# Second-layer chunk attention: its sixteen heads placed among the q, k, v and output products

## The chip, the cores and the metric

One core of one Trainium2 chip. The metric is device time in microseconds (us) of the whole kernel, median of the runs; lower is better.

## The reference, cut to what matters

Three layers run one after the other on 256 tokens of width 1024: two layers of a first block, then one layer of a second block on 272 tokens. Each has a mixer and a feed-forward network. The change is in the mixer of the second layer, which is chunk attention with 16 heads of 64:

```python
def chunk_band_mixer(u, w_qkv, rel_bias, w_out):
    qkv = (u @ w_qkv).reshape(bsz, n_chunks, CHUNK, 3, C_HEADS, C_DIM)
    q, k, v = qkv[:, :, :, 0], qkv[:, :, :, 1], qkv[:, :, :, 2]
...
    scores = scores + bias.astype(jnp.float32)[None, None]
    p = jax.nn.softmax(jnp.where(valid[None, :, None, None, :], scores, -jnp.inf), axis=-1).astype(v.dtype)
...
    return o.reshape(bsz, seq, MIX_ODD) @ w_out
h = h + chunk_band_mixer(u, od_w_qkv[i], od_rel_bias[i], od_w_out[i])
u = rms_norm(h, g_ffn[layer])
h = h + swiglu(u, w_gate[layer], w_up[layer], w_down[layer])
```

With 256 tokens all earlier chunks lie within reach, so a query sees every key of its own chunk of 64 and of those before. The bias depends on head and distance.

## The kernel before, in words

**Products.** Every weight matrix is cut into units of 1024 x 256. SP loads a unit into one of four `raw` slots; ScalarE (ACT) rounds it to `w_hi` (`split_hi`, L344) and VectorE (DVE) takes the rest as `w_lo` (`split_lo`, L353), each two units ahead of TensorE (PE). `product` (L492 to L494) does three fp32r matmuls for one k-tile: high by high, high by low, low by high. A unit is 2 output halves x 8 k-tiles x 3 = 48 matmuls of 256 columns. I call the three matmuls of one k-tile and half a group; a unit has 16.

**Order.** Each engine runs its own list in the order in which it is written, and semaphores tie the lists. A wait holds back all that stands behind it on its engine. `Phase` numbers the units and says which pair of PSUM banks each writes. `pair_read` counts its evictions, `unit_done` the units, `xl_done` the finished low parts of the moving operand.

**Second mixer.** `ph_qk` (8 units) makes q and k feature-major, evicted by DVE through `scaled` (L938). `ph_v` (4 units) makes v token-major, evicted by ACT (L1329). Then `chk`, an `Attention` object, does the 16 heads alone. Per head: GpSimd (POOL) copies 64 rows of q into the zeroed `q_pad_c` (L793); PE does two fp32 score matmuls and adds the chunk mask to each by a small bf16 matmul (L804, L807); DVE adds the bias (L1797, L1799), takes maxima (L727) and negates (L731); ACT does two exponentials with row sums (L681); DVE takes reciprocals (L740); PE transposes three blocks (L639); ACT copies them (L690); PE multiplies by v (three blocks of 64 columns, L648); ACT writes the scaled output (L699). When all heads are done PE turns the output feature-major with 16 transposes (`turn_pe`, L878), ACT and DVE split it (`o_hi`, `o_lo`), and `ph_out1`, 4 units, multiplies by the output weights.

**Output products.** `residual_dve` and `residual_act` go with `ph_out0` (first layer) and `ph_out1`. After unit k DVE adds it to `h` (L915), ACT makes the high part of the next input (`late_hi`, L925), DVE the low part (`late_lo`, L933), ACT squares (L966), and only then ACT and DVE split the next weights. The feed-forward's first unit needs the bank pair of unit 3. `fold_squares` (POOL, L418) adds up the squares and `late_sums` (PE, L435) sums them over features between the feed-forward's first and second unit.

## Time and profile before

| | us |
|---|---|
| median of 3 runs | 1218.66 (1216.96 to 1220.9) |
| profiled execution, its own time | 1217.98 |
| its span | 1216.2 |
| PE busy in it | 1152.9 |
| DVE, ACT, POOL busy | 784.1, 578.2, 55.5 |
| mean granted TensorE clock | 0.973 |

Busy times are sums over the span. Since PE is busy nearly throughout, the length of a stage is read from the chain that ended last, and a change has to be followed to what PE waits for. Times below are from the span's start.

### The profile page before, as it was taken

Reading aid. Unit: us, or ns where it says so; the run is one execution under the profiler, and the core shown is the slowest. Engines: PE = TensorE matmul, PEld = TensorE weight load, DVE = VectorE, ACT = ScalarE, POOL = GpSimd, SP = SyncE. Lnnn points to the kernel's source line nnn. Section 1 sums busy time; section 2 is a strip of 40 time slices with the busy share of each in tenths; the row PEclk is TensorE's granted clock in tenths of the full one; section 3 lists DMA queues with packets and bytes.
Section 4 is the critical chain, followed back from the end, with each engine's and each line's share of the span. In section 5 each row is a group of like instructions: output and inputs, shape, how many; then the busy total and the mean of one; then the engine's idle time right before and its main releaser. Section 6 shows DMA issues by size and latency. Waiting matters only on the chain.

```text
span 1216.2 us, 22867 instructions
## 1 busy us (share of the span) xinstructions
PE 1152.9 (95%) x9061; PEld 1110.9 (91%) x9061; DVE 784.1 (64%) x1224; ACT 578.2 (48%) x838; POOL 55.5 (5%) x82
## 2 busy tenths in 40 slices
PE   5998899999999999999999899999899998999998
PEld 4997899999999979999999799888687998999997
DVE  4546655655655475555555587989887666778743
ACT  4546654444444376444444443332355636565531
POOL 0003010000010020000000000100200000000000
PEclk9999799999999999999999998989898999999999
DMA  7662055654578512565546464333320544555360
GB/s 226 204 187 70 12 162 186 195 165 141 181 257 260 174 35 88 164 200 174 162 157 202 135 178 153 112 119 96 121 74 32 166 151 138 177 168 185 124 211 36
DMA packets 190773, 181.74 MB, mean 149 GB/s; under 512 B 20911, under 2 KB 189116, under 8 KB 190699
## 3 DMA queue, kind: packets, MB, share of 16 engines
q1 hardware_dynamic: 190171, 178.61, 46.4%
q0 software_dynamic: 528, 2.10, 0.6%
q8 instruction: 52, 0.85, 0.3%
q14 instruction: 22, 0.18, 0.0%
HBM read 179.64 MB, written 1.05 MB: 149 GB/s over the span
## 4 chain that ended last, share of the span: by engine, by line
PE 83%; DVE 9%; ACT 5%; issue 1%; DMA 1%; SPq 1%; POOL 0%; DVEq 0%; ACTq 0%; POOLq 0%
PE ps L492 24%; PE ps L493 24%; PE ps L494 24%; PE ps L648 3%; DVE w_lo L353 3%; DVE work L1830 2%; PE ps L804 2%; ACT w_hi L344 2%; PE ps L639 1%; PE ps L878 1%; DMA conv_rows<-in_conv_dw_w 1%; PE ps L1636 1%; PE ps L401 1%; ACT u_hi L925 0%; DVE rope L851 0%
## 5 line engine op out<-in xcount | busy, mean ns | idle before, releaser
L492 PE MATMUL ps<-u_hi,w_hi 128*128 128x256 f32 (+2 forms) x1864 | 534.4, 287 | 18.4 <-DVE u_lo L461 8.7
L493 PE MATMUL ps<-u_lo,w_hi 128*128 128x256 f32 (+2 forms) x1864 | 531.2, 285 | 0.0
L494 PE MATMUL ps<-u_hi,w_lo 128*128 128x256 f32 (+2 forms) x1864 | 530.2, 284 | 0.0
L353 DVE TENSOR_TENSOR w_lo<-raw,w_hi 128x2048 fp32r<-128x2048 f32 (+5 forms) x184 | 385.1, 2101 | 205.2 <-ACT w_hi L344 204.9
L492 PEld LDWEIGHTS ps<-u_hi,w_hi 128*128 128x128 f32 x1864 | 356.6, 191 | 21.5 <-issue 14.8
L494 PEld LDWEIGHTS ps<-u_hi,w_lo 128*128 128x128 f32 x1864 | 356.7, 191 | 0.0
L493 PEld LDWEIGHTS ps<-u_lo,w_hi 128*128 128x128 f32 x1864 | 356.1, 191 | 0.5
L344 ACT ACTIVATE w_hi<-raw 128x2048 fp32r<-128x2048 f32 (+5 forms) x184 | 319.7, 1754 | 48.1 <-PE ps L494 48.1
L493 PE MATMUL ps<-a_lo,w_hi 128*128 128x256 f32 x528 | 148.3, 281 | 0.0
L494 PE MATMUL ps<-a_hi,w_lo 128*128 128x256 f32 x528 | 147.9, 280 | 0.0
L492 PE MATMUL ps<-a_hi,w_hi 128*128 128x256 f32 x528 | 147.3, 279 | 0.1
L492 PEld LDWEIGHTS ps<-a_hi,w_hi 128*128 128x128 f32 x528 | 99.5, 188 | 0.3 <-DVE w_lo L353 0.3
L1830 DVE SCALAR_TENSOR_TENSOR work<-cin,conv_w,work 128x258 f32<-128x258 f32 x240 | 99.6, 487 | 0.0
L494 PEld LDWEIGHTS ps<-a_hi,w_lo 128*128 128x128 f32 x528 | 99.5, 188 | 0.0
L493 PEld LDWEIGHTS ps<-a_lo,w_hi 128*128 128x128 f32 x528 | 99.2, 188 | 0.0
L418 POOL TENSOR_TENSOR work<-work 128x512 f32<-128x512 f32 (+1 forms) x15 | 19.6, 1307 | 733.3 <-ACT work L961 462.4
L991 ACT ACTIVATE a_hi<-act_a 128x512 f32 (+1 forms) x22 | 13.9, 632 | 74.2 <-DVE act_a L1011 74.2
L988 ACT ACTIVATE act_g<-act_g 128x512 f32<-128x512 f32 x22 | 13.9, 632 | 60.1 <-DVE act_g L938 60.1
L961 ACT ACTIVATE work<-h (+2 forms) x24 | 9.0, 417 | 70.3 <-DVE h L915 70.3
L494 PE MATMUL ps<-w_hi,u_lo 128*128 128x256 f32 (+1 forms) x136 | 38.7, 285 | 0.0
L493 PE MATMUL ps<-w_lo,u_hi 128*128 128x256 f32 (+1 forms) x136 | 38.7, 285 | 0.0
L995 DVE TENSOR_TENSOR a_lo<-act_a,a_hi 128x512 f32 (+1 forms) x33 | 22.8, 691 | 24.4 <-ACT a_hi L991 19.0
(266 smaller groups left out, 1305.0 us busy)
## 6 DMA issues: line engine op xcount, KB each, us to landing
raw<-in_w_in SPq DMA_DIRECT2D x24, 1024.0 KB, 5.4
raw<-in_w_gate SPq DMA_DIRECT2D x22, 1024.0 KB, 5.3
raw<-in_w_up SPq DMA_DIRECT2D x22, 1024.0 KB, 5.3
raw<-in_ffn_up SPq DMA_DIRECT2D x22, 1024.0 KB, 5.0
raw<-in_w_down SPq DMA_DIRECT2D x16, 768.0 KB, 4.7
raw<-in_od_w_qkv SPq DMA_DIRECT2D x12, 1024.0 KB, 7.5
raw<-in_w_down SPq DMA_DIRECT2D x16, 640.0 KB, 4.6
raw<-in_ev_w_in SPq DMA_DIRECT2D x8, 1024.0 KB, 8.1
```

Of the source, the lines that this page charges most:

```text
L344: nc.scalar.activation(w_hi[t % RING][:, 0:n], raw[t % RAW][:, 0:n], ACT.Copy).then_inc(hi_done, 1)
L353: nc.vector.tensor_tensor(w_lo[t % RING][:, 0:n], raw[t % RAW][:, 0:n], w_hi[t % RING][:, 0:n].bitcast(F32), ALU.subtract).then_inc(lo_don ...
L418: nc.gpsimd.tensor_tensor(first, first, paired(work)[:, j, :, 0:n], ALU.add).then_inc(sem("sq_folded"), 1)
L492: nc.tensor.matmul(out_ap, a_h, b_h, start=start and n == 0, stop=False)
L493: nc.tensor.matmul(out_ap, a_h, b_l, start=False, stop=False)
L494: mm = nc.tensor.matmul(out_ap, a_l, b_h, start=False, stop=stop and n == len(pairs) - 1)
L648: mm = nc.tensor.matmul(self.O(e, b), self.PT(e, b, key), v(n, e, b, key), start=key == 0, stop=key == len(keys) - 1)
L804: nc.tensor.matmul(out_ap, lhs, rhs, start=t == 0, stop=False)
L988: nc.scalar.activation(act_g[:, s], act_g[:, s], ACT.Silu).then_inc(sem("silu_done"), 1)
L991: nc.scalar.activation(paired(a_hi)[:, j], act_a[:, s], ACT.Copy).then_inc(sem("ffn_hi"), 1)
L995: nc.vector.tensor_tensor(paired(a_lo)[:, j], act_a[:, s], paired(a_hi)[:, j].bitcast(F32), ALU.subtract)\
L1830: nc.vector.scalar_tensor_tensor(out=work[:, tile, 0:NF], in0=src, scalar=tap, in1=work[:, tile, 0:NF], op0=ALU.mult, op1=ALU.add).then_in ...
```

## The change

The twelve units of q, k and v become one phase `ph_qkv` in the order q, k, v for each group of four heads, and the heads are written into the lists at positions counted in groups of three matmuls: position 16k is where unit k begins, 192 is the first output unit. `CK_HEADS` gives a head's scores (40, 52, 64, 76, 88, ... 172, then 184, 192, 200, 208), `CK_TURNS` its transposes (18 positions later, 15 for the last four), `CK_VALUES` its values (4 more). Each other engine has the same loop over positions x with its own share. Units 1 to 11 use one PSUM bank each. The chunk mask is added to the bias table once by POOL, and the mask matmuls go. POOL also normalises the probabilities (two `tensor_scalar` a head). Values are multiplied with v as the stationary operand, padded with zeros to 128 columns (`v_even`, `v_odd`), so that the output comes feature-major and the 16 transposes go. The first three output units run their k-tiles 0 to 5 first, with heads between, and their tiles 6 and 7 together at the end; unit 3 follows. Additions, splits and squares there have an order of their own. `residual_act` in the first layer's `ph_out0` splits the next weights before the late part, and does the late part one unit behind.

```diff
-    ph_qk = Phase(plan, 8, 4, first=1)
-    ph_v = Phase(plan, 4, 4)
+    ph_qkv = Phase(plan, 12, 12, pairs=3)
...
+    GROUPS = 2 * KT
+    EARLY = 2 * (KT - 2)
+    def ck_start(k):
+        return GROUPS * k if k < 12 else GROUPS * 12 + EARLY * (k - 12)
+    CK_HEADS = [GROUPS * (3 * (n // 4) + 2) + 8 + (12 if n < 12 else 8) * (n % 4) for n in range(C_H)]
+    CK_TURNS = [at + (18 if n < 12 else 15) for n, at in enumerate(CK_HEADS)]
+    CK_VALUES = [at + 4 for at in CK_TURNS]
+    CK_END = CK_VALUES[-1] + 4
+    CK_STARTS = {ck_start(k): k for k in range(15)}
+    def due(table, x, late=0):
+        return [n for n, at in enumerate(table) if at + late == x]
...
+        def late_part(i, k, j):
+            for t in range(2):
+                added(i, k, j, t)
+                late_hi(late, j, t)
+            for t in range(2):
+                squares(j, t)
+        one_behind = late is not None and group == 1
         for i, k in ph.steps(nc.scalar):
             split_hi(ph, i, k)
-            if k % group == group - 1:
+            if one_behind:
+                if k:
+                    late_part(i, k - 1, k - 1)
...
-        pairs_read(pool, ph_v)
-        pad_heads(chk, q_c, q_pad_c)
+        nc.gpsimd.memset(v_odd[:], 0.0).then_inc(sem("v_zeroed"), 1)
+        pool.wait_ge(sem("v_zeroed"), 1)
+        pool.wait_ge(sem("ss_done"), norm_at["mix1"][0] + 1)
+        nc.gpsimd.memset(v_even, 0.0).then_inc(sem("v_zeroed"), 1)
+        pool.wait_ge(sem("v_zeroed"), 2)
+        pool.wait_ge(sem("bias_landed"), 16)
+        own = bias_h[:, :, 0:P]
+        nc.gpsimd.tensor_tensor(own, own, c("chunk_mask")[:, ::-1].unsqueeze(1).to_broadcast([P, C_H, P]), ALU.add)\
+            .then_inc(sem("bias_masked"), 1)
+        pool.wait_ge(sem("bias_masked"), 1)
+        def ck_pad(n):
+            k = 3 * (n // 4)
+            pool.wait_ge(pair_read[ph_qkv.pair(k)], ph_qkv.used_before(0, k) + 1)
+            wait(pool, sem("ck_scores"), n - 3)
+            rows = slice(64 * (n % 2), 64 * (n % 2) + 64)
+            nc.gpsimd.tensor_copy(q_pad_c[rows, n % 4, :], q_c[rows, n // 2, :]).then_inc(sem("ck_pad"), 1)
+            pool.wait_ge(sem("ck_pad"), n + 1)
+        ck_pad(0)
+        for n in range(C_H):
+            if n + 1 < C_H:
+                ck_pad(n + 1)
+            pool.wait_ge(sem("ck_rsum"), n + 1)
+            for b, (lo, hi) in enumerate(CK_SPANS):
+                nc.gpsimd.tensor_scalar(p3[:, n % 2, lo:hi], p3[:, n % 2, lo:hi], stat3[:, n % 4, 3, b:b + 1], None, ALU.mult)\
+                    .then_inc(sem("ck_norm"), 1)
+                pool.wait_ge(sem("ck_norm"), 2 * n + b + 1)
...
+        def ck_v(k):
+            g, p = k // 3, ph_qkv.pair(k)
+            act.wait_ge(unit_done, ph_qkv.unit(0, k) + 1)
+            act.wait_ge(sem("v_zeroed"), 2)
+            act.wait_ge(sem("tok_copied"), 1)
             for b in range(2):
-                a = nc.scalar.activation(v_c[:, b, k * UC:(k + 1) * UC], ps[:, 2 * p + b, 0:UC], ACT.Copy, scale=rstd_tok[:, b:b + 1])
+                src = qkv_banks(k)[:, b, :].rearrange("p (j e d) -> p j e d", j=2, e=2)
+                for e, v in enumerate((v_even, v_odd)):
+                    a = nc.scalar.activation(v[:, b, 2 * g:2 * g + 2, HD * e:HD * e + HD], src[:, :, e, :], ACT.Copy,
+                                             scale=rstd_tok[:, b:b + 1])
...
+        for x in range(CK_END):
+            if (k := CK_STARTS.get(x)) is not None and k < 14:
+                if k and k % 3 == 0:
+                    ck_v(k - 1)
+                split_hi(ph_qkv if k < 12 else ph_out1, 0, k if k < 12 else k - 12)
+                if k == 0:
+                    late_roots("mix1")
+            for n in due(CK_HEADS, x, 5):
+                ck_exps(n)
+            for n in due(CK_TURNS, x, 1):
+                ck_copies(n)
+            for n in due(CK_VALUES, x, 1):
+                if n % 2:
+                    ck_out_hi(n // 2)
...
+        split_hi(ph_out1, 0, 2)
+        for j in range(3):
+            out1_hi(j)
+        split_hi(ph_out1, 0, 3)
+        out1_squares(0)
+        out1_hi(3)
+        for j in range(1, 4):
+            out1_squares(j)
...
+        def ck_scores(n):
+            k = 3 * (n // 4) + 1
+            pe.wait_ge(pair_read[ph_qkv.pair(k)], ph_qkv.used_before(0, k) + 1)
+            pe.wait_ge(sem("ck_pad"), n + 1)
+            wait(pe, sem("ck_biased"), n - 1)
+            nc.tensor.matmul(ck_bank(n)[:, 0:P], q_pad_c[:, n % 4, 0:P], k_c[:, n // 2, 0:P], start=True, stop=True)
+            nc.tensor.matmul(ck_bank(n)[:, P:CK_W], q_pad_c[:, n % 4, P:T1], k_c[:, n // 2, :], start=True, stop=True)\
+                .then_inc(sem("ck_scores"), 1)
+        def ck_turns(n):
+            pe.wait_ge(sem("ck_norm"), 2 * n + 2)
+            wait(pe, sem("ck_ptc"), n)
+            for at in range(0, CK_W, P):
+                mm = nc.tensor.transpose(ps[:, 5, at:at + P], p3[:, n % 2, at:at + P], ident)
+            mm.then_inc(sem("ck_pt"), 1)
+        def ck_values(n):
+            j, k, v = n // 2, 3 * (n // 4) + 2, v_odd if n % 2 else v_even
+            pe.wait_ge(pair_read[ph_qkv.pair(k)], ph_qkv.used_before(0, k) + 1)
+            pe.wait_ge(sem("tok_copied"), 1)
+            pe.wait_ge(sem("ck_ptc"), n + 1)
+            if j >= 2:
+                pe.wait_ge(sem("xl_done"), split_at["o1"] + j - 1)
+            out_ap = ps[:, 6 + j % 2, 0:T1]
+            every, later = (out_ap, v[:, 0, j, :], pt3[:, n % 2, 0:T1]), (out_ap[:, P:T1], v[:, 1, j, :], pt3[:, n % 2, T1:CK_W])
+            nc.tensor.matmul(*(later if n % 2 else every), start=n % 2 == 0, stop=False)
+            nc.tensor.matmul(*(every if n % 2 else later), start=False, stop=n % 2 == 1).then_inc(sem("ck_o"), 1)
+        def ck_steps(x):
+            for n in due(CK_TURNS, x):
+                ck_turns(n)
+            for n in due(CK_VALUES, x):
+                ck_values(n)
+            for n in due(CK_HEADS, x):
+                ck_scores(n)
...
+        pairs_read_after = [ph_qkv.used_after[n] for n in range(3)]
+        for k in range(3):
+            begin_unit(ph_out1, 0, k)
+            for t in range(2):
+                if k == 0:
+                    pe.wait_ge(pair_read[t], pairs_read_after[t])
+                elif k == 1 and t == 0:
+                    pe.wait_ge(pair_read[2], pairs_read_after[2])
+                elif k == 1:
+                    pe.wait_ge(sem("ck_biased"), C_H - 1)
+                elif t == 0:
+                    pe.wait_ge(sem("ck_biased"), C_H)
+                else:
+                    pe.wait_ge(sem("xl_done"), split_at["o1"] + KT - 1)
+                for kt in range(KT - 2):
+                    ck_steps(ck_start(12 + k) + t * (KT - 2) + kt)
+                    pe.wait_ge(sem("xl_done"), split_at["o1"] + kt + 1)
+                    out1_group(k, kt, t)
+        for kt in (KT - 2, KT - 1):
+            pe.wait_ge(sem("xl_done"), split_at["o1"] + kt + 1)
+            for k in range(3):
+                for t in range(2):
+                    mm = out1_group(k, kt, t)
+                if kt == KT - 1:
+                    mm.then_inc(unit_done, 1)
+        begin_unit(ph_out1, 0, 3)
...
+        for x in range(CK_END):
+            if (k := CK_STARTS.get(x)) is not None and 0 < k <= 12 and k % 3:
+                ck_qk(k - 1)
+            if (k := CK_STARTS.get(x - 6)) is not None and k < 14:
+                split_lo(ph_qkv if k < 12 else ph_out1, 0, k if k < 12 else k - 12)
+            for n in due(CK_HEADS, x, 1):
+                ck_maxima(n)
+            for n in due(CK_HEADS, x, 9):
+                ck_rsum(n)
+            for n in due(CK_VALUES, x, 2):
+                if n % 2:
+                    ck_out_lo(n // 2)
...
+        out1_added(0)
+        out1_added(1)
+        split_lo(ph_out1, 0, 2)
+        out1_lo(0)
+        out1_added(2)
+        out1_lo(1)
+        out1_lo(2)
+        out1_added(3)
+        out1_lo(3)
+        split_lo(ph_out1, 0, 3)
```

**POOL, at the end of the first feed-forward.** Rows are the line, the operation, output<-inputs and what it waits for. `work` in the third memset is `v_even`. Before:

```order
L418 TENSOR_TENSOR work<-work 128x2x256 [waits sq_folded,sq_done] x5
L1185 DMA bias_h<-in_od_rel_bias 128x16x256 [waits pair_read2,pair_read3,pair_read1,pair_read0]
L1186 MEMSET q_pad_c 128x1024
L793 COPY q_pad_c<-qk_c 64x256 [waits pair_read3,pair_read2,at_scores,pair_read1,pad_done,pair_read0,zeroed]
L793 COPY q_pad_c<-qk_c 64x256 [waits pad_done,at_scores] x3
```

The same place of the changed kernel:

```order
L1231 DMA bias_h<-in_od_rel_bias 128x16x256 [waits pair_read2,pair_read3,pair_read1,pair_read0]
L1232 MEMSET q_pad_c 128x1024
L1234 MEMSET v_odd 128x2048 [waits zeroed]
L1237 MEMSET work 128x2048 [waits ss_done,v_zeroed]
L1242 TENSOR_TENSOR bias_h<-bias_h,const 128x16x128 [waits bias_landed,v_zeroed]
L1251 COPY q_pad_c<-qk_c 64x256 [waits pair_read0,bias_masked]
L1251 COPY q_pad_c<-qk_c 64x256 [waits pair_read0,ck_pad]
L1260 TENSOR_SCALAR p<-p,stat 128x128 [waits ck_rsum,ck_pad]
L1260 TENSOR_SCALAR p<-p,stat 128x256 [waits ck_norm]
```

The first head's query copy now stands behind the landing of the bias and a pass over 2048 elements of it.

**DVE, around a head's reciprocal.** Before, the q and k phase has nothing between a product's eviction and the next split:

```order
L938 TENSOR_TENSOR qk_c<-ps,rstd 128x512 [waits unit_done]
L353 TENSOR_TENSOR w_lo<-raw,w_hi 128x2048 [waits hi_done]
L938 TENSOR_TENSOR qk_c<-ps,rstd 128x512 [waits unit_done]
L353 TENSOR_TENSOR w_lo<-raw,w_hi 128x2048 [waits hi_done]
L938 TENSOR_TENSOR qk_c<-ps,rstd 128x512 [waits unit_done]
```

In the changed kernel, at a v unit: the fourth head of one group, and the first of the next:

```order
L2010 TENSOR_REDUCE stat<-biased 128x1
L2013 TENSOR_SCALAR stat<-stat 128x2 [waits ck_max]
L969 TENSOR_TENSOR qk_c<-ps,rstd 128x512 [waits rstd_done,unit_done]
L2018 RECIPROCAL stat<-stat 128x2 [waits ck_p]
L355 TENSOR_TENSOR w_lo<-raw,w_hi 128x2048 [waits hi_done]
L2005 SCALAR_TENSOR_TENSOR biased<-ps,bias_h 128x128 [waits ck_p,bias_masked,ck_scores]
```

A weight split now stands right behind the reciprocal that lets POOL normalise.

**ACT, where a v unit ends.** Before:

```order
L1329 ACTIVATE v_c<-ps,rstd_tok 128x256 [waits unit_done]
L1329 ACTIVATE v_c<-ps,rstd_tok 128x256
L344 ACTIVATE w_hi<-raw 128x2048 [waits unit_done,raw_landed3]
L1329 ACTIVATE v_c<-ps,rstd_tok 128x256 [waits unit_done]
L1329 ACTIVATE v_c<-ps,rstd_tok 128x256
```

In the changed kernel, from the eviction of a group's v:

```order
L1400 ACTIVATE work<-ps,rstd_tok 128x2x64 [waits tok_copied,v_zeroed,unit_done]
L1400 ACTIVATE v_odd<-ps,rstd_tok 128x2x64
L1400 ACTIVATE work<-ps,rstd_tok 128x2x64
L1400 ACTIVATE v_odd<-ps,rstd_tok 128x2x64
L346 ACTIVATE w_hi<-raw 128x2048 [waits unit_done,raw_landed3]
L1420 ACTIVATE o_hi<-ps 128x256 [waits ck_o]
L1409 ACTIVATE p,stat<-biased,stat 128x128 [waits ck_rsum,ck_pt,ck_neg]
L1409 ACTIVATE p,stat<-biased,stat 128x256
L1416 ACTIVATE pt<-ps 128x384 [waits ck_o,ck_pt]
```

The rounding of a head pair's output now stands behind four evictions and a weight split.

## Rows read from the trace of the kernel before

**Rows 1.** The page's chain that ended last, by engine.

```profile
PE 83%; DVE 9%; ACT 5%; issue 1%; DMA 1%; SPq 1%; POOL 0%; DVEq 0%; ACTq 0%; POOLq 0%
```

**Rows 2.** The chain in order of time around the heads: start, us, what.

```profile
425.97 0.13 PE ps L494
465.20 0.12 PE ps L492
```

**Rows 3.** The chain through one head in mid-stage, same columns.

```profile
434.52 0.28 PE ps L804 x2
...
434.85 0.49 PE ps L804 x2
...
435.39 0.33 PE ps L639 x3
435.73 0.62 PE ps L648 x6
```

**Rows 4.** The chain at late_sums, and where the third q unit begins.

```profile
362.55 0.86 PE ps L435 x4
...
369.31 0.12 PE ps L492
```

**Rows 5.** Windows, PE: stretch, its length, busy, granted clock, DMA share, GB/s.

```profile
461.70:465.30 3.60, 3.60 (x19) 0.55 0.00 0
```

**Rows 6.** Timeline of POOL, and the DMA issue's us to landing (last number).

```profile
361.14 1.29 POOL L1185 DMA_DIRECT2D bias_h<-in_od_rel_bias  x1
362.43 0.97 POOL L1186 MEMSET q_pad_c<- 128x1024 f32 x1
...
bias_h<-in_od_rel_bias POOLq DMA_DIRECT2D x1, 2048.0 KB, 11.4
```

**Rows 7.** POOL's groups by form: busy us, mean ns, idle before.

```profile
L418 POOL TENSOR_TENSOR work<-work 128x512 f32<-128x512 f32 x13 | 17.0, 1308 | 626.0 <-ACT work L961 355.0 <-ACT work L966 271.0
...
L793 POOL COPY q_pad_c<-qk_c 64x256 f32 x12 | 4.7, 396 | 14.7 <-PE ps L807 14.4 <-POOL q_pad_c L793 0.4
```

**Rows 8.** Timelines of POOL and DVE at 92 us.

```profile
92.28 2.36 POOL L793 COPY q_pad<-q_nope 64x256 f32<-64x256 f32 x1
...
92.08 2.29 DVE L353 TENSOR_TENSOR w_lo<-raw,w_hi 128x2048 fp32r<-128x2048 f32 x1 [0.39 <-ACT w_hi L344]
```

**Rows 9.** PE after its idle 4.24 us: timeline, then the chain.

```profile
1014.89 0.56 PE L492 MATMUL ps<-u_hi,w_hi 128*128 128x258 f32 x1 [4.24 <-DVE u_lo L461]
...
1017.81 0.21 PE ps L492
```

**Rows 10.** One head's DVE and ACT parts, timeline.

```profile
456.05 0.29 DVE L1797 SCALAR_TENSOR_TENSOR biased<-ps,bias_h 128x128 f32<-128x128 f32 x1 [0.35 <-PE ps L807]
...
457.56 0.40 ACT L681 ACTIVATE p<-biased,stat 128x128 f32<-128x128 f32 x1 [0.16 <-DVE stat L731]
...
458.45 0.49 ACT L699 ACTIVATE work<-ps,stat 128x64 f32 x2
```

**Rows 11.** ACT's eviction of a v unit, timeline.

```profile
409.09 0.84 ACT L1329 ACTIVATE v_c<-ps,rstd_tok 128x256 f32<-128x256 f32 x2 [9.35 <-PE ps L494]
```

**Rows 12.** PE's waits over the whole span: us in total, times, longest.

```profile
PE ps L492 <- DVE w_lo L353: 4.3, 3, 2.0
```

**Rows 13.** End of the second output product, timelines of ACT and DVE.

```profile
483.40 0.91 ACT L925 ACTIVATE u_hi<-h,gains 128x256 fp32r<-128x256 f32 x2 [2.69 <-DVE h L915]
484.22 0.71 ACT L966 ACTIVATE work<-h 128x256 f32<-128x256 f32 x2
484.83 1.91 ACT L344 ACTIVATE w_hi<-raw 128x2048 fp32r<-128x2048 f32 x1
...
486.77 2.29 DVE L353 TENSOR_TENSOR w_lo<-raw,w_hi 128x2048 fp32r<-128x2048 f32 x1 [1.94 <-ACT w_hi L344]
488.98 0.75 DVE L915 TENSOR_TENSOR h<-h,ps 128x256 f32<-128x256 f32 x2
489.97 0.89 DVE L933 SCALAR_TENSOR_TENSOR u_lo<-h,gains,u_hi 128x256 fp32r<-128x256 f32 x2 [0.24 <-ACT u_hi L925]
```

More of the change, by code:

```diff
@@ L36 @@
 DOWN_WIDTHS = [n * UC for _ in range(D // UC) for _, n in DOWN_KT]
+CK_W = 3 * P
 BLOCKS1 = [(0, P, [(0, P)]), (P, P, [(0, P), (P, P)])]
@@ L1330, in _, with ck_exps @@
             a.then_inc(pair_read[p], 1)
-        chk.act(1.0, lambda e, b: biased_ap(e, b))
-        turn_act(KT, T1, o_hi)
-        residual_act(ph_out1, C1, late="ffn1")
+        def ck_exps(n):
+            act.wait_ge(sem("ck_neg"), n + 1)
+            wait(act, sem("ck_pt"), n - 1)
+            wait(act, sem("ck_rsum"), n - 3)
+            for b, (lo, hi) in enumerate(CK_SPANS):
+                a = nc.scalar.activation(p3[:, n % 2, lo:hi], biased[:, n % 2, lo:hi], ACT.Exp,
+                                         bias=stat3[:, n % 4, 1, b:b + 1], accum_out=stat3[:, n % 4, 2, b:b + 1])
+            a.then_inc(sem("ck_p"), 1)
@@ new lines, in out1_added, with out1_lo @@
+        def out1_added(j):
+            p = ph_out1.pair(j)
+            dve.wait_ge(unit_done, ph_out1.unit(0, j) + 1)
+            for t in range(2):
+                hv = paired(h)[:, j, t, C1]
+                nc.vector.tensor_tensor(hv, hv, out1_bank(j, t), ALU.add).then_inc(pair_read[p] if t else sem("half_added"), 1)
+        def out1_lo(j):
+            for t in range(2):
+                late_lo("ffn1", j, t)
+        out1_added(0)
+        out1_added(1)
+        split_lo(ph_out1, 0, 2)
```

203 lines of the change are left out of this document (128 added, 75 removed).

## The prediction

> **What bounds the kernel now.** I read the page's chain first: PE is 83% of it [rows 1], so a microsecond is won only where PE runs a matmul fewer or stands still for less. Then the chain in order of time around the heads. The last matmul of the v product ends at 426.10 and the first of the output product starts at 465.20 [rows 2]: the heads and the turning of their output keep the weight products waiting for 39.1 us. Within that, a head's pieces follow each other on PE: scores 0.28 and 0.49, transposes 0.33, values 0.62, and two mask matmuls of about 0.06 [rows 3]. So PE works for most of the stage, and what can be hidden is small. The rest is a start (first scores wait for v and for POOL), an end (last softmax, then 16 transposes), and a slow stretch: at 461.7 to 465.3, where the transposes run, the granted clock is 0.55 [rows 5], mostly the lower of the two levels, 1.2 GHz. Last I read the PE waits: three on a weight split, 4.3 us in all, the longest 2.0 [rows 12]. Two of them lie where the output product of a layer meets its feed-forward, and each is about 2.0.
>
> **The stage removed, the work added.** Removed: 39.1 us. Added on PE per head: two score matmuls and two value matmuls, each pair 128 + 256 columns in fp32, and three transposes. The nearest row for fp32 work set between fp32r products is the sum of squares: four passes over 256 columns take 0.86, 0.215 each, with nothing lost at the change of type [rows 4]. A fp32 matmul is two passes, so 384 columns cost 0.645, twice, plus 0.33 for the transposes [rows 3]: 1.62 a head, 26.0 for 16. By the stage's own rows it would be 0.28 + 0.49 = 0.77 for a pair, 1.87 a head, 29.9. I take 26.5, near the first, since the surroundings are those. So far -39.1 + 26.5 = -12.6.
>
> **The first head waits for POOL.** The second unit begins where the sum of squares ends, 363.41, and the third at 369.31 [rows 4]; less some 0.2 for two small transposes between, 48 matmuls take 5.7, one 0.118, a group of three 0.353. Position 40, eight groups into the third unit, is at 372.1. There PE wants the first copy of q. POOL issues the bias load at 361.14 and it lands 11.4 us later, at 372.5 [rows 6]. The memsets (0.97 for 1024 elements [rows 6], so 1.9 each for 2048) are over by 367.3 and hide in that. Then comes the mask addition, 2048 elements: four times a fold of 512, 1.308 [rows 7], gives 5.2, so 377.8; the copy 0.40 [rows 7] and some 0.1 to reach PE make 378.3. PE stands still for 6.2 us. Everything behind it on PE, half a weight unit among it, waits too; ACT and DVE are ahead already and gain nothing. Bounds: if the pass went at the rate of the one-input copy (256 in 0.396, 3.2 for 2048) the stall is 4.2; if a weight split holds POOL once (below) it is 8.5. After an idle of 4.24 us, from 1014.89 to about 1017.8, PE ran 13 matmuls at 0.215 in place of 0.12 [rows 4, 9], 1.2 us lost, at the lower clock level. The idle here is longer, so I take 1.8 (1.2 to 3). Together +8.0.
>
> Beside the row stands the Trainium skill, GPSIMD Engine Reference, Performance versus the Vector engine: it gives a two-input add of 2048 fp32 elements 4.50 us. By it the pass ends 0.7 earlier and the stall is 5.5; no run here shows that size yet.
>
> **POOL against the weight splits.** One POOL copy took 2.36 where the others of its kind took 0.40. It began at 92.28, and DVE was in a weight split from 92.08 to 94.37 [rows 8]: POOL got through when the split was over. The same reference page says in its Specifications that POOL's SBUF interface is shared with VectorE and contended by DVE instructions with two SBUF inputs; the trace agrees, with 2.36 against 0.40. By the row POOL now stands in each head's path, twice, where a split can hold it. Where it bites follows from the lists. In steady state DVE's reciprocal has a split right behind it for one head in four (the fourth of a group). From scores to transposes PE does 18 groups and 1.6 us of other heads' work, 8.0 us. Needed are DVE 1.5 and ACT 0.9 [rows 10], reciprocal 0.2, a held 2.3, two normalisations of about 0.8 and hops of 0.5: 6.2, plus what queues before it, about 1.5. Just hidden, at zero. In the last four heads scores are 8 positions apart, transposes follow after 15, and the split stands between head 14's reciprocal and its transposes: its maxima start late behind head 15's, and PE waits about 1.9.
>
> **ACT's queue.** At the end of a v unit ACT has four evictions of 128 elements, about 1.1 in all (two of 256 take 0.84 [rows 11]), then a split of 1.9, and only then the rounding of the last pair's output. DVE's low part waits for that, the next head's maxima wait for DVE, its exponentials follow, and the copy of the first head's transposes stands behind them. Laid out with these durations the copy is ready some 0.65 after PE wants it, in two groups of four: +1.3 (0 to 3). At position 197 the sixth k-tile of the output product needs the same rounding: the values end 2.0 after the last v unit, ACT is free at 3.1, the two halves take 0.9, PE wants it at 2.7: +1.4. With the 1.9 above the tail costs 3.3 (0 to 5).
>
> **Into the feed-forward.** Before, unit 3's addition stood behind a split that ended at 489.06, and PE stood still about 2.0 [rows 12, 13]. Now splits come behind additions, but units 0 to 2 finish within 1.4 us of each other, and DVE has three additions, a split and three late parts to do (0.75 x 3 + 2.3 + 0.89 x 3 = 7.2 after the first, with a first wait of 0.4 for ACT) against 7.0 until unit 3 ends. The gap comes to 1.5: -0.5. The squares of the last three pairs, however, come only after everything else, at 12.4 after unit 0; before, two of three folds were long done. Three folds of 1.3 in a row end at 15.0, PE has finished the feed-forward's first unit at 14.1. If DVE's split holds the first fold, 2.7 instead of 0.9. I take +1.8, late squares being what is late next.
>
> **First layer's output product.** Before, a round is 0.75 for the addition, 0.91 and 0.71 for ACT's late part and squares, 1.91 and 2.29 for the splits [rows 13], 6.0 with overlap against PE's 5.65. Now the ACT split is done before the addition, so the round on DVE alone is about 4.1, and the gap of 2.0 at its end shrinks to the addition and hops, 1.0: -1.0.
>
> Sum: -12.6 + 8.0 + 3.3 + 1.3 - 0.5 + 1.8 - 1.0 = +0.3. The profiled execution's own time is 1217.98, its span 1216.2; it lies 0.7 below the median 1218.66. So 1218.3 for such an execution, 1219.0 as a median. Not touched: weight traffic (same units, same 1 KB rows), all other stages.
>
> **The rivals.**
> 1. The heads hide as laid out (likeliest): within 0.3% of before, 0.41. A measurement tells about 0.3% (3.7 us) from no change.
> 2. Faster: the queue waits of ACT and POOL are not there, because ACT splits weights before PE gets to them and POOL slips in ahead of DVE. Then only the first stall remains, at its low end: -12.6 + 4.2 + 1.2 - 0.5 + 0.9 - 1.0 = -7.8, or with the stall as computed -5.2: 1211 to 1213.5. For it speaks that a unit with its 1.33 heads takes 5.7 + 1.33 x 1.65 = 7.9 on PE, and DVE is busy for about 2.3 + 0.5 + 1.33 x 1.9 = 5.3 of it, ACT for 1.9 + 0.4 + 1.33 x 1.6 = 4.4. Against it: all four engines are now in one ring of waits in fixed order. 0.31.
> 3. Slower: POOL's normalisation is late in steady state. Its place is the wait before a head's transposes. I left 0.3 of slack for the fourth head of a group; if the two `tensor_scalar` cost 2 us more with their semaphores, or if reads are held in every head by the splits that have drifted, PE waits 1.5 at each of the four-in-sixteen and about 0.4 at the others: 4 x 1.5 + 12 x 0.4 = +10.8, 1230; at half of that 1224.4. It decides for slower once these waits pass 3.4 us in all. 0.28.
> 4. That nothing happens is no rival: the stage of 39.1 is gone by the order of the lists. But the stall could vanish if the bias landed by 367; then -8.0 comes off and the time is 1211, which is inside rival 2.
>
> **How the numbers follow.** The likeliest is rival 1 with its sum, 1219.0; its own range, from the bounds of its terms taken together, is 1215 to 1222. Rival 2 reaches down to 1211, rival 3 up to 1230; leaving out a tenth at either end gives 1211.5 to 1225. Faster 0.31, same 0.41, slower 0.28, from the same cases.
>
> **What would show it right or wrong.** A single PE wait near 372 to 378, ended by POOL's copy, 6.2 long, then matmuls at 0.21 for some microseconds. POOL's mask addition near 5.2. No idle in PE longer than 1 us between 378 and the last q, k, v unit; a wait near 1.4 at the start of the output product and one of 1.9 before head 14's transposes. POOL normalisations that last 2.3 more where they meet a split. The feed-forward of the second layer starting 8.0 - 12.6 + 4.6 - 0.5 - 1.0 = 1.5 us earlier than at 489.83, and its second unit 1.8 late again. In the first layer a gap of 1.0, not 2.0. The prediction fails if the mask pass is short, if PE's fp32 work costs nearer 1.87 a head, or if waits of half a microsecond stand before most transposes or values.

## The result

| | before | changed |
|---|---|---|
| median, range (20 runs each) | 1217.91 us, 1214.88 to 1220.90 | 1220.05 us, 1216.99 to 1223.74 |
| ratio to before, 95% interval | | 1.0021, 1.0013 to 1.0030 |
| profiled execution: own time, span | 1217.98, 1216.2 us | 1219.72, 1217.9 us |

By the ratio the change costs 2.6 us (1.6 to 3.7 by the interval; the medians differ by 2.1), which is within the 0.3% that counts as no change. Predicted were 1219.0 and "the same" as the likeliest.

The page's chain of the changed kernel, by engine, answers to [rows 1]:

```profile
PE 81%; DVE 7%; issue 4%; ACT 3%; DMA 2%; POOL 2%; SPq 1%; ACTq 0%; DVEq 0%; POOLq 0%
```

DMA and POOL were 1% and 0% there. Why they have come into it, PE's waits show, from 140 to 520 us of the changed kernel (us in total, times, longest):

```profile
PE ps L1687 <- POOL q_pad_c L1251: 5.9, 1, 5.9
PE ps L437 <- POOL work L420: 4.2, 1, 4.2
PE ps L1695 <- POOL p L1260: 2.5, 2, 2.2
PE ps L494 <- issue: 1.9, 2, 1.0
PE ps L1687 <- issue: 0.8, 1, 0.8
PE ps L494 <- DVE o_lo L2022: 0.7, 1, 0.7
```

The stage of heads, 39.1 us in [rows 2], is gone, and PE waits instead at these six entries, eight times in all. The first three entries are all for POOL. L1687 is the first head's scores, L437 the sums of squares of the feed-forward, L1695 the transposes of heads. The two waits of L494 of about 1.0 stand where [rows 12] had 2.0 each: an output product against its feed-forward, in both layers.

Where the heads run, windows of the changed kernel (stretch, its length, busy time of PE, PEld, DVE, ACT and POOL, granted clock, DMA share, GB/s):

```profile
371.00:376.00 5.00, 0.17 (x1) 0.20 (x2) 0.00 (x0) 0.00 (x0) 4.88 (x3) 0.59 1.10 348
376.00:392.00 16.00, 16.00 (x119) 15.66 (x120) 8.91 (x20) 8.62 (x20) 4.00 (x7) 0.91 0.28 94
392.00:448.00 56.00, 55.72 (x443) 54.39 (x442) 34.97 (x73) 29.44 (x65) 23.53 (x28) 1.00 0.41 133
448.00:478.00 30.00, 26.00 (x202) 24.73 (x201) 11.48 (x29) 11.92 (x30) 11.85 (x13) 1.00 0.35 106
493.00:501.00 8.00, 3.92 (x14) 3.56 (x15) 2.20 (x2) 1.75 (x3) 3.89 (x2) 0.61 0.81 254
```

Read it in parts. In the middle, 392 to 448, PE is busy for 55.72 of 56 us, at the full clock: all of a head but its matmuls is hidden. What is lost lies at the start (371 to 376, where PE, DVE and ACT do next to nothing and POOL is busy), in the last four heads (26.00 of 30), and after the output product (3.92 of 8, at 0.61).

To compare single traces I use one stretch from here on: from the sums of squares in front of the q, k, v product to the eleventh gate product of the second layer's feed-forward. All of the change but its part in the first layer lies in it, and what the clock does elsewhere stays out. Its ends before:

```profile
362.39 1.02 PE L435 MATMUL ps<-work,const 128*128 128x256 f32 x4
...
609.90 0.69 DVE L938 TENSOR_TENSOR act_g<-ps,rstd 128x512 f32<-128x512 f32 x1 [0.84 <-PE ps L494]
```

and in the changed kernel:

```profile
360.20 1.02 PE L437 MATMUL ps<-work,const 128*128 128x256 f32 x4
...
613.62 0.69 DVE L969 TENSOR_TENSOR act_g<-ps,rstd 128x512 f32<-128x512 f32 x1 [0.85 <-PE ps L496]
```

That is 247.5 before and 253.4 now: 5.9 longer. Ahead of it the changed trace is 2.2 shorter, of which 1.1 is the first layer's gap (2.0 to 0.9); behind it, it is 2.0 shorter, though the instructions there are the same (the last section tells how that can be). 5.9 - 2.2 - 2.0 = 1.7, the difference of the two profiled executions.

### The profile page after: what moved, and what is told of

It is laid out like the page before. It is cut to its first block, busy times and chain, and to the rows that moved or that the text cites. A ratio compares the mean times of both kernels' runs of the same rounds, so it can differ in the third digit from the quotient of the medians.

```text
span 1217.9 us, 22533 instructions
## 1 busy us (share of the span) xinstructions
PE 1145.1 (94%) x8981; PEld 1104.1 (91%) x8981; DVE 783.7 (64%) x1228; ACT 573.7 (47%) x818; POOL 107.3 (9%) x117
## 4 chain that ended last, share of the span: by engine, by line
PE 81%; DVE 7%; issue 4%; ACT 3%; DMA 2%; POOL 2%; SPq 1%; ACTq 0%; DVEq 0%; POOLq 0%
PE ps L494 24%; PE ps L495 24%; PE ps L496 24%; PE ps L650 2%; DVE w_lo L355 1%; DVE work L2083 1%; PE ps L803 1%; DMA bias_h<-in_od_rel_bias 1%; PE ps L641 1%; PE ps L909 1%; DMA conv_rows<-in_conv_dw_w 1%; ACT w_hi L346 1%; POOL work L420 1%; PE ps L403 1%; PE ps L1848 1%
## 5 line engine op out<-in xcount | busy, mean ns | idle before, releaser
L494 PE MATMUL ps<-u_hi,w_hi 128*128 128x256 f32 (+2 forms) x1864 | 538.2, 289 | 17.0 <-DVE u_lo L463 8.7
L494 PEld LDWEIGHTS ps<-u_hi,w_hi 128*128 128x128 f32 x1864 | 357.8, 192 | 20.3 <-issue 17.1
L494 PE MATMUL ps<-a_hi,w_hi 128*128 128x256 f32 x528 | 147.0, 278 | 0.1
L494 PEld LDWEIGHTS ps<-a_hi,w_hi 128*128 128x128 f32 x528 | 99.3, 188 | 0.3 <-DVE w_lo L355 0.3
L420 POOL TENSOR_TENSOR work<-work 128x512 f32<-128x512 f32 (+1 forms) x15 | 27.0, 1801 | 706.7 <-ACT work L987 688.1
L987 ACT ACTIVATE work<-h 128x256 f32<-128x256 f32 (+2 forms) x40 | 14.6, 411 | 71.8 <-DVE h L946 71.8
L494 PE MATMUL ps<-w_hi,u_hi 128*128 128x256 f32 (+1 forms) x136 | 39.8, 293 | 0.0
L494 PE MATMUL ps<-o_hi,w_hi 128*128 128x256 f32 x128 | 37.6, 294 | 0.7 <-DVE o_lo L2022 0.7
```

What stands on the lines that cost most here:

```text
L420: nc.gpsimd.tensor_tensor(first, first, paired(work)[:, j, :, 0:n], ALU.add).then_inc(sem("sq_folded"), 1)
L494: nc.tensor.matmul(out_ap, a_h, b_h, start=start and n == 0, stop=False)
L987: nc.scalar.activation(paired(work)[:, j, t, 0:n], paired(h)[:, j, t, cols], ACT.Square)\
```

## The experiments

The first four shared a chip (before there 1218.43 us, 35 runs), the next four another (1217.97, 23 runs), the last three a third (1218.26, 11 runs). All are compared with their own runs of before.

| kernel | median us (runs) | ratio to before (95%) | stretch, us |
|---|---|---|---|
| changed | 1220.05 (20) | 1.0021 (1.0013 to 1.0030) | 253.4 |
| e1_pad_first | 1216.29 (11) | 0.9987 (0.9978 to 0.9997) | 249.4 |
| e2_squares_early | 1216.43 (12) | 0.9982 (0.9970 to 0.9995) | 253.4 |
| e3_norm_dve | 1216.12 (12) | 0.9989 (0.9975 to 1.0004) | 250.3 |
| e4_out0_only | 1216.88 (12) | 0.9979 (0.9963 to 0.9995) | 248.6 |
| f1_fold_guard | 1218.63 (12) | 1.0001 (0.9986 to 1.0017) | 249.4 |
| f2_mask_on_pe | 1216.90 (12) | 0.9995 (0.9986 to 1.0005) | 249.3 |
| f3_pad_norm_guard | 1208.73 (6) | 0.9921 (0.9900 to 0.9941) | 242.7 |
| f4_mask_norm_guard | 1207.99 (6) | 0.9930 (0.9911 to 0.9950) | 240.5 |
| g1_later_start | 1224.91 (6) | 1.0054 (1.0035 to 1.0074) | 259.8 |
| g2_turns_14 | 1227.47 (6) | 1.0085 (1.0063 to 1.0107) | 260.3 |
| g3_f4_squares | 1205.43 (6) | 0.9907 (0.9885 to 0.9928) | 241.2 |

The stretch of one trace is good to about 1 us: e4_out0_only has the instructions of before in it, and 248.6 against 247.5.

**e1_pad_first** takes the mask pass out of the first head's way, and leaves it in being.

```diff
+        ck_pad(0)
+        ck_pad(1)
         pool.wait_ge(sem("bias_landed"), 16)
         own = bias_h[:, :, 0:P]
         nc.gpsimd.tensor_tensor(own, own, c("chunk_mask")..., ALU.add)
...
-        ck_pad(0)
         for n in range(C_H):
-            if n + 1 < C_H:
+            if 0 < n < C_H - 1:
                 ck_pad(n + 1)
```

> The changed kernel with POOL's query copies for heads 0 and 1 ahead of the wait for the bias and of the mask addition. Theory (the copy is late only because it is queued behind them, and the bias itself is wanted later): PE's wait of 5.9 before the first scores and its half-clock matmuls behind it are gone. Head 0's maxima still wait for the mask (375.2), so its transposes come 2 to 2.5 late. Net 4 to 6 us faster than the changed kernel, 1214 to 1216 (ratio to before 0.997 to 0.9985). Rival (the stall only moves to the next thing that needs the bias): under 1.5 us gained, one wait of 5 or more before head 0's transposes.

The first stall is gone, and the first head's transposes wait 2.16 us in its place, as expected: the maxima need the masked table. The stretch fell by 4.0, the ratio by 0.34%, the low end of what was expected. So the stall comes from the order of POOL's list. What it is made of, the changed kernel's POOL shows, timeline:

```profile
358.95 1.35 POOL L1231 DMA_DIRECT2D bias_h<-in_od_rel_bias  x1
360.30 0.98 POOL L1232 MEMSET q_pad_c<- 128x1024 f32 x1
361.34 1.82 POOL L1234 MEMSET v_odd<- 128x2048 f32 x1
363.21 1.82 POOL L1237 MEMSET work<- 128x2048 f32 x1
370.75 4.49 POOL L1242 TENSOR_TENSOR bias_h<-bias_h,const 128x2048 f32<-128x2048 f32 x1 [5.71 <-DMA bias_h<-in_od_rel_bias]
375.30 0.85 POOL L1251 COPY q_pad_c<-qk_c 64x256 f32<-64x256 f32 x2
```

The memsets are over at 365.03, and POOL idles 5.71 us for the table. The pass then takes 4.49, and the copy, 0.4 long, is all that PE wants.

**e2_squares_early** puts each piece's squares right behind its high part on ACT, so that the folds come earlier.

```diff
         for j in range(3):
             out1_hi(j)
+            out1_squares(j)
         split_hi(ph_out1, 0, 3)
-        out1_squares(0)
         out1_hi(3)
-        for j in range(1, 4):
-            out1_squares(j)
+        out1_squares(3)
```

> The changed kernel with ACT's squares of output units 0 to 2 right behind each high part, ahead of the next weight split. Theory (the folds are late because the squares are, and two of them run into DVE's splits and are held): folds 1 and 2 take 1.3 each and are over before PE ends the feed-forward's first unit; only fold 3 meets a split, PE waits 0.2 to 0.6 in place of 4.2, and its clock stays at the upper level. 5 to 6.5 us faster than the changed kernel, about 1214.5 (ratio 0.997). Rival (ACT is the bound there, 2.1 us of squares ahead of the split push the second unit's weights out): PE waits for weights about 2 us, gain under 3 us.

PE's wait for the sums, 4.2, is gone, and the ratio fell by 0.39%, less than the 5 to 6.5 us expected. The first two folds are free, as expected, but PE waits 2.4 at the entry of the feed-forward, in place of 1.0. The timelines of POOL and of DVE in this kernel say why:

```profile
487.11 1.31 POOL L420 TENSOR_TENSOR work<-work 128x512 f32<-128x512 f32 x1 [14.50 <-issue]
489.24 1.40 POOL L420 TENSOR_TENSOR work<-work 128x512 f32<-128x512 f32 x1 [0.81 <-ACT work L1447]
492.89 3.17 POOL L420 TENSOR_TENSOR work<-work 128x512 f32<-128x512 f32 x1 [2.25 <-ACT work L1447]
...
487.85 3.08 DVE L964 SCALAR_TENSOR_TENSOR u_lo<-h,gains,u_hi 128x256 fp32r<-128x256 f32 x4
...
492.63 5.58 DVE L355 TENSOR_TENSOR w_lo<-raw,w_hi 128x2048 fp32r<-128x2048 f32 x2
```

The hold goes both ways. DVE's four late parts take 3.08 where the same four in the changed kernel take 1.67: the first of them began beside the first fold and took 0.87, the last beside the second fold and took 1.50, against about 0.48 each. The third fold begins in a split and takes 3.17; and the two splits, 2.29 each by themselves, take 5.58, since the second began beside that fold and took 3.37. Whichever came first kept its pace, and the other waited. That DVE loses by it was in no expectation. In the trace the stretch didn't get shorter at all: after its first stall (6.6 here) the granted clock was 0.80 from 376 to 392, against 0.91, and it was 0.89 from 460 to 476, against 1.00 there. The median of 12 runs is the better witness here.

**e3_norm_dve** moves the two `tensor_scalar` that normalise a head's weights from POOL to DVE, behind the reciprocal.

```diff
         nc.vector.reciprocal(stat3[:, n % 4, 3, :], ...).then_inc(sem("ck_rsum"), 1)
+        dve.wait_ge(sem("ck_rsum"), n + 1)
+        for b, (lo, hi) in enumerate(CK_SPANS):
+            nc.vector.tensor_scalar(p3[:, n % 2, lo:hi], p3[:, n % 2, lo:hi], stat3[:, n % 4, 3, b:b + 1], None, ALU.mult)...
```

> The changed kernel with the two normalisations of a head on DVE, right behind the reciprocal, in place of POOL. Theory (POOL's normalisation is held by weight splits and costs PE 2.5 us before two of the last heads' transposes, nothing elsewhere): those waits go, about 0.5 us more DVE work per head stays hidden; 2 to 3 us faster than the changed kernel, about 1217.5 (ratio 0.9985 to 1.0005). Rival (DVE is the tighter engine now that it also splits and evicts): waits appear before values or transposes in every group of four, no gain or slower.

The two waits before transposes (0.3 and 2.2) and the 0.8 before head 15's scores are gone; the first stall (6.2) and the wait for the sums (4.2) stand. The stretch fell by 3.1, the ratio by 0.32%, as expected. The wait before head 15's scores was POOL's too: in the changed kernel a split holds the copy of that head's q, on POOL's timeline:

```profile
455.84 2.06 POOL L1251 COPY q_pad_c<-qk_c 64x256 f32<-64x256 f32 x1
```

Other copies of this form take 0.39.

**e4_out0_only** is the kernel before, with the new order of DVE and ACT in the first layer's output product alone.

> The kernel before, with only the new order of ACT's steps in the first layer's output product (weights split first, late part one unit behind). Theory: PE's gap of 2.0 at the end of that product becomes about 0.9, 1.0 to 1.2 us faster than before (ratio 0.999). Rival (the gain is given back at the feed-forward's square sums): ratio 1.000, and a new wait before the sums.

The gap at that product's end is 0.9, not 2.0, and the second layer's is still 2.0. The median gives 1.5 us, the ratio 2.6 with a wide interval (0.6 to 4.5). The trace's 1.1 lies in it.

**f1_fold_guard** adds one wait. It was made to tell whether POOL's folds of 3.1 us are held by DVE's splits or are slow for a reason of their own.

```diff
         out1_lo(3)
+        dve.wait_ge(sem("sq_folded"), folded["ffn1"] + 3)
         split_lo(ph_out1, 0, 3)
```

> The changed kernel with one wait more: VectorE waits for GpSimd's three folds of the second output product's squares before it begins the splits of the last turned pieces, so no fold lies beside a split. If the splits hold the folds (my theory), the folds take about 1.3 us each instead of 3.14, 3.13 and 1.27, they end about 3.7 us earlier, TensorE's wait for the sums (4.2 us now, followed by about 2.3 us lost at half clock) falls to under 2 us, with a wait of about 1.5 us for the second unit's weights in its place, and the kernel is about 4 us faster than the changed one (1216, ratio to before about 0.998). Rival: the folds are slow for a reason of their own; then they keep 3.1 us, the splits begin later, and the kernel is 0 to 3 us slower than the changed one (1220 to 1223).

POOL and DVE in the changed kernel, timelines:

```profile
489.23 7.80 POOL L420 TENSOR_TENSOR work<-work 128x512 f32<-128x512 f32 x3 [18.36 <-issue]
...
488.92 2.28 DVE L355 TENSOR_TENSOR w_lo<-raw,w_hi 128x2048 fp32r<-128x2048 f32 x1
492.16 2.34 DVE L355 TENSOR_TENSOR w_lo<-raw,w_hi 128x2048 fp32r<-128x2048 f32 x1 [0.96 <-ACT w_hi L346]
500.23 0.69 DVE L969 TENSOR_TENSOR act_g<-ps,rstd 128x512 f32<-128x512 f32 x1 [5.72 <-ACT rstd L446]
```

and with the wait:

```profile
491.23 4.16 POOL L420 TENSOR_TENSOR work<-work 128x512 f32<-128x512 f32 x3 [18.35 <-issue]
...
495.42 4.49 DVE L355 TENSOR_TENSOR w_lo<-raw,w_hi 128x2048 fp32r<-128x2048 f32 x2 [4.43 <-POOL work L420]
```

Three folds take 4.16, about 1.3 each with 0.14 between them, in place of 7.80. DVE stands idle for 4.43 us before its splits, and still the stretch is 4.0 shorter, as expected. The ratio is 0.20% lower (0.02 to 0.38 from the two intervals), where 0.4% was expected: of the whole kernel's gain the runs show no more than that it is there. PE waits 0.6 for the sums, and 1.2 for the second unit's weights, not 4.2. So the folds were held.

**f2_mask_on_pe** undoes one part of the change: the chunk mask is added by PE again, by two bf16 matmuls a head, and POOL's pass is left out.

```diff
-        nc.gpsimd.tensor_tensor(own, own, c("chunk_mask")..., ALU.add)...
...
+            nc.tensor.matmul(ck_bank(n)[:, 0:P], ident_b, chunk_b, start=False, stop=True)
...
+            nc.tensor.matmul(ck_bank(n)[:, 2 * P:CK_W], ident_b, chunk_b, start=False, stop=True)\
```

> The changed kernel with the chunk mask back on TensorE, as 32 bfloat16 matmuls of 128 columns, and without GpSimd's pass over the bias table; VectorE waits for the table's transfer instead. If the pass alone makes the stall in front of head 0's scores, the 5.9 us wait and the 1.5 us at half clock behind it go, the masks add 32 times 0.055 = 1.8 us of TensorE's work, and the kernel is about 5.5 us faster than the changed one (1214.5, ratio to before 0.997). Rival: the stall is the bias table's transfer and only moves to VectorE's wait for it; then TensorE waits 2 us or more at head 0's transposes and the gain is 2 us or less (1218 and above).

The stall is gone and none came in its place at head 0, so the transfer alone (issued at 359.02) was early enough. The stretch fell by 4.2 and the ratio by 0.26%, less than the 5.5 us expected: with its masks the scores of a head put off the next product's second matmul by 0.87 (393.30 to 394.29, less one 0.12), without them by 0.65. That is 3.5 for 16 heads and not 1.8.

**f3_pad_norm_guard** and **f4_mask_norm_guard** put the parts together: the first e1, e3 and f1, the second f2, e3 and f1.

> The changed kernel with three edits: GpSimd's query copies for heads 0 and 1 ahead of the mask pass, the normalisation of the weights on VectorE, and VectorE waiting for the folds before the last splits. If the stalls are independent, the gains add: about 4 us from the first stall (as measured for that edit alone), 2 to 4 us from the normalisation, 4 us from the folds: 1208 to 1211, ratio to before about 0.993. Rival: what one removes returns in another place (VectorE, now with the normalisation as well, becomes what TensorE waits for): 1214 to 1217, as with one edit alone.

> As the kernel before it in this list, but with the mask on TensorE as 32 small matmuls instead of GpSimd's pass. Against that kernel it saves the wait of about 2.2 us at head 0's transposes and pays 1.8 us of mask matmuls: within 1 us of it, 1208 to 1211. If the pass on GpSimd is cheap once it is hidden, this is slower than it by 1 to 2 us.

The gains add: singly 4.0 + 3.1 + 4.0 = 11.1 in the stretch, together 10.7; the medians are 1208.73 and 1207.99, by the ratios 0.7 to 0.8% below before. Between the two the intervals can't decide. The stretch says 2.2 for the second, whose PE waits from 355 to 475 us are one:

```profile
PE ps L494 <- DVE o_lo L2017: 0.5, 1, 0.5
```

**g1_later_start** moves the table of positions only.

```diff
-    CK_HEADS = [GROUPS * (3 * (n // 4) + 2) + 8 + (12 if n < 12 else 8) * (n % 4) for n in range(C_H)]
+    CK_HEADS = [48 + 11 * n if n < 12 else 184 + 8 * (n - 12) for n in range(C_H)]
```

> The changed kernel with the first twelve heads at positions 48, 59, 70, ... (eleven apart) in place of 40, 52, 64, ... (twelve apart); the last four stay where they are. TensorE then does eight groups of products more, 2.8 us, before it wants GpSimd's first copy of q. If the first stall is a date (GpSimd's chain from the issue of the bias load) and nothing that runs along, it falls from 5.9 to about 3.1 us, less is lost at half clock behind it, and the kernel is about 3.5 us faster than the changed one (1216.5, ratio to before 0.9985). Rival: at eleven apart the heads' loop through four engines no longer fits, and waits before transposes and values appear in steady state: 1220 to 1226.

Both halves came true, and the second outweighs the first: the stretch is 6.4 longer. PE's waits, 355 to 480 us:

```profile
PE ps L1707 <- ACT pt L1416: 4.8, 3, 2.5
PE ps L1687 <- POOL q_pad_c L1251: 3.3, 1, 3.3
```

The stall fell to 3.3 (3.1 expected), but values now wait three times for ACT's copy. The longest of them, on ACT:

```profile
427.96 0.37 ACT L1400 ACTIVATE work<-ps,rstd_tok 128x128 f32<-128x128 f32 x1 [0.64 <-PE ps L496]
...
428.97 1.93 ACT L346 ACTIVATE w_hi<-raw 128x2048 fp32r<-128x2048 f32 x1
430.77 0.51 ACT L1416 ACTIVATE pt<-ps 128x384 f32<-128x384 f32 x1
```

The copy stands behind the four evictions of a v unit and a split, 2.8 us. In the changed kernel the same copy (head 7's) runs at 427.13, just ahead of the evictions at 427.83. The prediction's ACT queue has the same evictions and the same split in it, but at its end another copy, that of the next head. PE's waits in the stretch are 2.6 longer in all. The rest lies mostly in the clock: from 424 to 440 and from 476 to 492 it was 0.89, in the changed kernel 1.00 in both, which makes 3.5 us if those shares were spent at half clock.

**g2_turns_14** takes 4 groups, 1.4 us, of cover from each of the first twelve heads.

```diff
-    CK_TURNS = [at + (18 if n < 12 else 15) for n, at in enumerate(CK_HEADS)]
+    CK_TURNS = [at + (14 if n < 12 else 15) for n, at in enumerate(CK_HEADS)]
```

> The changed kernel with a head's transposes 14 positions behind its scores in place of 18 (values 4 behind these, as before), for the first twelve heads. That takes 4 groups, 1.4 us, from the time in which softmax runs under TensorE's other work, which leaves about 6.6 us. My working has 6.2 us needed plus about 1.5 of queueing, for the heads that meet a weight split: so waits of about 1 us before the transposes of one head in four and perhaps 0.3 elsewhere, 3 to 6 us slower than the changed kernel (1223 to 1226). If the steady state has real slack, nothing changes (1219 to 1221). If rival 3 of the prediction is right, and all heads are near their limit, about 1.4 us at each of twelve heads is lost: 1230 and above.

PE's waits for the normalisation, 377 to 472 us:

```profile
PE ps L1695 <- POOL p L1260: 7.7, 4, 3.0
```

Three of the four are 1.56 each, at 404.00, 429.30 and 454.60, the last head of each group of four; the fourth, 3.0 at 464.10, is head 12's, whose normalisation a split holds too (3.69 at 460.36), which it doesn't in the changed kernel. The total, 6.8 in the stretch and 1227.5, is above my 1223 to 1226, mostly by the 3.0 that I hadn't followed.

The 1.56 isn't the price of 1.41 of cover alone. In the changed kernel the same heads have 1.5 us to spare (see "Steady state" below), so a pure loss of 1.41 would just have fitted. But the table also sets the order on ACT. The copy of the head before (head 2's here) now comes ahead of a weight split, and head 3's exponentials behind both:

```profile
396.91 0.49 ACT L1416 ACTIVATE pt<-ps 128x384 f32<-128x384 f32 x1 [3.42 <-PE ps L1695]
397.30 1.91 ACT L346 ACTIVATE w_hi<-raw 128x2048 fp32r<-128x2048 f32 x1
399.11 0.39 ACT L1409 ACTIVATE p<-biased,stat 128x128 f32<-128x128 f32 x1
```

In the changed kernel that split runs from 393.72, ahead of the copy, and the exponentials begin at 396.31. From head 3's scores to its normalisation it is 5.4 us here and 3.7 there. What less cover alone would cost isn't shown.

**g3_f4_squares** is f4 with e2's edit on top.

> The kernel with the mask on TensorE, the normalisation on VectorE and the wait for the folds, now with each turned piece's squares on ScalarE right behind its high part, too. The folds begin about 2 us earlier, so VectorE's splits do as well, and the waits for the sums (0.6) and for the second unit's weights (1.2) go: about 1.5 us faster than without it (1206.5). Rival: the folds then lie beside VectorE's late parts and hold them (as with the early squares alone, where four of them took 3.08 us in place of 1.67), so that TensorE waits 1 to 1.5 us more at the entry of the feed-forward: the same time, 1208.

Both things happened: the waits for sums (0.6) and weights (1.2) are gone, and the entry's wait is 2.5, with DVE's four late parts at 3.07. The median, 1205.43, is 2.6 below f4's, the stretch 0.6 above it; the intervals overlap. Whether it is faster than f4 stays open. It beats before by 0.9% (0.7 to 1.2).

## Why the prediction was right, and where not

The forecast of no change held, 1219.0 against 1220.05 as a median (before was 1218.66 in the runs that it started from, 1217.91 in those beside the changed kernel). Rivals 2 and 3 didn't come about. The mechanism was mostly right, but that the number came so near is luck in part: a change of +0.3 was forecast, the ratio says +2.6 (1.6 to 3.7), and one term was off by 4.7 us, of which other terms and the clock elsewhere gave part back. In the order of the prediction:

| term | predicted | measured |
|---|---|---|
| stage removed | -39.1 | -39.1 (read from before) |
| fp32 work of the heads in PE | +26.5 | +27.4 |
| first stall, clock behind it | +6.2, +1.8 | +5.9, +1.5 |
| last heads | +3.3 | +4.0 |
| ACT's queue | +1.3 | +0.3 |
| into the feed-forward | -0.5 | -1.0 |
| late squares and sums | +1.8 | +6.5 |
| first layer's gap | -1.0 | -1.1 |
| sum | +0.3 | +4.4 |

**The heads' work on PE.** For eight heads from 392 to 440 us I took what each start of a matmul lies behind the last, less the 0.118 of a product and the short waits: 13.7, or 1.71 a head, for 16 heads 27.4. The rows chosen (four passes of the sums of squares) were the right neighbours, and the stage's own rows (1.87) the wrong ones.

**The first stall.** 5.9 against 6.2. The bias load took 11.7 from issue to landing (11.4 before) and was issued at 358.95, 2.2 earlier than before, like everything here. The pass took 4.49, where I scaled the fold's row to 5.2. The Trainium skill, GPSIMD Engine Reference, Performance versus the Vector engine, gives 4.50 for that size; the trace agrees, with 4.49. Behind the stall PE ran at half clock, as its timeline shows, second column the duration, and the starts 0.21 apart until 378.74, then 0.12:

```profile
375.83 0.77 PE L1687 MATMUL ps<-qk_c,q_pad_c 128*128 128x128 f32 x2 [5.89 <-POOL q_pad_c L1251]
...
377.89 0.41 PE L494 MATMUL ps<-w_hi,u_hi 128*128 128x256 f32 x1
378.11 0.41 PE L495 MATMUL ps<-w_lo,u_hi 128*128 128x256 f32 x1
...
378.98 0.28 PE L494 MATMUL ps<-w_hi,u_hi 128*128 128x256 f32 x1
```

**Steady state.** A head's normalisation on POOL takes 1.62 when free, and the prediction had two operations of about 0.8: right. Its sum of what a head needs counts them only once, though. With both it is 7.0 and not 6.2, and with the 1.5 of queueing 8.5, more than the 8.0 that it had. A split holds the normalisation in one head of four (3.51 at 397.66, 421.62 and 445.57), as the prediction placed it. But "just hidden, at zero" isn't what the trace has. The fourth head's scores start at 393.95. POOL and PE, timelines:

```profile
397.66 3.51 POOL L1260 TENSOR_SCALAR p<-p,stat 128x128 f32<-128x128 f32 x2 [2.76 <-DVE stat L2018]
```

```profile
402.64 0.38 PE L1695 MATMUL ps<-const,p 128*128 128x128 f32 x2
```

The weights are ready 7.2 us after the scores and wanted after 8.7: 1.5 to spare in these heads, 1.8 to 3.3 in the others of the first twelve. Rival 3 stayed away by that margin. It decides from 3.4 us of waits in all; g2_turns_14, with 7.7, shows that four positions less, and the order that comes with them, are enough for it.

**ACT's queue** cost 0.3, not 1.3. The chain is there as the prediction laid it out, evictions, split, rounding, DVE's low part, the next head's maxima and exponentials, and last the copy of head 4's transposes. DVE, ACT and PE, timelines:

```profile
407.12 0.42 DVE L2022 TENSOR_TENSOR o_lo<-ps,o_hi 128x256 fp32r<-128x256 f32 x1 [3.72 <-ACT o_hi L1420]
```

```profile
409.85 0.47 ACT L1416 ACTIVATE pt<-ps 128x384 f32<-128x384 f32 x1
```

```profile
410.58 0.46 PE L1707 MATMUL ps<-pt,work 128*128 128x256 f32 x1
```

PE stands still for 0.14 before that last row, and again at 434.53 for head 8: two groups of four, as predicted, but 0.14 each and not 0.65. g1_later_start shows what it costs when other copies fall behind a weight split on ACT, 4.8 in three places.

**The tail.** Before head 14's transposes PE waits 2.2 (predicted 1.9), at the sixth k-tile of the output product 0.7 (1.4), and 0.8 before head 15's scores (a held copy, see e3_norm_dve), which I didn't have; another 0.3 before head 13's transposes. e3_norm_dve removes all of these but the 0.7, so they hang on POOL.

**Late squares and sums** is the term that was mis-sized. The mechanism stood in the prediction (folds at the end, the first of them held by a split). The step that failed is "if DVE's split holds the first fold, 2.7 instead of 0.9. I take +1.8": it holds two folds (3.1 us each), since the second begins at 492.50, when DVE is in the next split since 492.16, and the wait is 4.2. And PE then ran at half clock here too, 11 matmuls 0.21 apart and the sums in 2.08 in place of 1.02, about 2.3 us lost, which I had counted at the first stall and forgot here. Together that is 6.5. It can be checked on PE's first matmul of the feed-forward, before and in the changed kernel:

```profile
489.83 0.36 PE L492 MATMUL ps<-u_hi,w_hi 128*128 128x256 f32 x1 [2.01 <-DVE w_lo L353]
```

```profile
487.00 0.35 PE L494 MATMUL ps<-u_hi,w_hi 128*128 128x256 f32 x1 [1.02 <-issue]
```

From there to the end of the stretch (609.90 and 613.62) it is 120.07 us before and 126.62 now: 6.5 or 6.6. f1_fold_guard, with 122.39, gets 4.2 of it back by one wait.

The measured terms sum to +4.4, and the stretch with the first layer gives 5.9 - 1.1 = 4.8: all but 0.4 of what the stretch lost is in a named term. Outside of both the changed trace is another 3.1 shorter (1.1 ahead, 2.0 behind), which is how 4.8 becomes the 1.7 of the two profiled executions; the ratio of the runs says 2.6.

## What to carry to other kernels

Work that is moved in among other work costs in its middle only what the busiest engine itself does for it (here 1.71 us a head on PE), and the rest of its price at the ends: look at the first piece (what must have landed), the last (what still queues behind it), and the thing after it (here the squares). A small operation on POOL that began beside VectorE's weight split was over only some time after the split (folds of 1.3 took 3.1); count how many passes can meet it, not whether one can, and remember that making VectorE idle until POOL is through can be the faster order. Moving one entry of a table of positions also changes the order on every other engine, as in g2_turns_14: read the trace before you take its result as the price of the distance. Price a long PE wait with the half clock behind it: here 1.5 us behind one of 5.9 and 2.3 behind one of 4.2.
